# Cached values of sample batches 3 to 7 loaded from the scalar engine's DMA queue in a two-layer streaming encoder step

## What is computed

```python
def attn_mixer_sample(h, ck, cv, cki, w_in, q_g, k_g, w_out):
    ...
    k_all = jnp.concatenate([ck, k], axis=1)
    v_all = jnp.concatenate([cv, v], axis=1)
    ki_all = jnp.concatenate([cki, ki], axis=1)
    k_sel = min(TOPK_MAX, (P + T) // 4)
    o = sparse_attend(q, qi, wi, pos, k_all, v_all, ki_all, k_sel)
    return o @ w_out, k, v, ki
```

## Time and profile before

| | |
|---|---|
| Time before, median of 3 runs | 1678.91 us (1678.46 to 1679.55) |
| Profiled execution, its own time | 1676.94 us |
| Span of its trace | 1675.0 us |
| PE busy | 1617.9 us, 97% of the span |
| DVE, ACT, POOL busy | 55%, 37%, 10% of the span |
| HBM read over the span | 136.29 MB |
| Scores of batch 0 begin | 219.58 us into the span |
| Scores of batch 7 begin | 269.87 us |
| Scores of prompt block 1 begin | 278.69 us |
| Last output transposed | 338.05 us |

### The profile page before, as it was taken

How to read it: one execution, slowest core, us unless ns; L and a number is a source line. 1 busy time by engine, 2 the same in 40 slices (tenths; PEclk the granted TensorE clock), 3 DMA queues, 4 the chain that set the end, 5 groups by cost and what they waited for, 6 DMA issues and landing times.

```text
span 1675.0 us, 25851 instructions
## 1 busy us (share of the span) xinstructions
PE 1617.9 (97%) x11138; PEld 1548.9 (92%) x11138; DVE 927.9 (55%) x1287; ACT 621.4 (37%) x928; POOL 168.1 (10%) x270
## 2 busy tenths in 40 slices
PE   7999878999999999999999999999999999999998
PEld 7759835799999999999999999999999999999998
DVE  5278877445665266526656715537663566346653
ACT  4546434734332133213354433324331233123441
POOL 2000000012110011001121100021110011001200
PEclk9999989999999999999999999999999999999999
DMA  5212445011222222221231221321222122211321
GB/s 217 80 50 77 153 179 201 26 58 69 76 76 76 76 76 72 80 76 56 75 112 70 92 83 55 113 76 64 72 72 95 52 76 76 101 51 63 114 92 48
DMA packets 27938, 143.52 MB, mean 86 GB/s; under 512 B 3392, under 2 KB 7104, under 8 KB 14640
## 3 DMA queue, kind: packets, MB, share of 16 engines
q1 hardware_dynamic: 26912, 139.03, 23.5%
q0 software_dynamic: 768, 2.81, 0.5%
q10 hardware_dynamic: 144, 0.02, 0.0%
HBM read 136.29 MB, written 5.43 MB: 85 GB/s over the span
## 4 chain that ended last, share of the span: by engine, by line
PE 92%; DVE 3%; ACT 2%; issue 1%; DMA 0%; SPq 0%; ACTq 0%; DVEq 0%
PE psum L634 71%; PE psum L680 9%; PE psum L720 2%; PE psum L551 1%; PE psum L490 1%; PE psum L583 1%; PE psum L499 1%; PE psum L590 1%; PE psum L538 1%; PE psum L669 1%; PE psum L510 1%; PE psum L565 1%; ACT a_hi L973 1%; DMA xT<-in_xT 0%; PE psum L759 0%
## 5 line engine op out<-in xcount | busy, mean ns | idle before, releaser
L634 PE MATMUL psum<-a_hi,w_hi 128*128 128x384 f32 (+2 forms) x1920 | 439.2, 310 | 7.5 <-DVE a_lo L1283 7.5
L634 PE MATMUL psum<-a_hi,w_lo 128*128 128x384 f32 (+2 forms) x1920 | 437.8, 309 | 0.0
L634 PE MATMUL psum<-a_lo,w_hi 128*128 128x384 f32 (+2 forms) x1920 | 437.7, 309 | 0.0
L634 PEld LDWEIGHTS psum<-a_hi,w_hi 128*128 128x128 f32 x1920 | 341.8, 188 | 9.6 <-issue 6.7
L634 PEld LDWEIGHTS psum<-a_hi,w_lo 128*128 128x128 f32 x1920 | 342.3, 188 | 0.0
L634 PEld LDWEIGHTS psum<-a_lo,w_hi 128*128 128x128 f32 x1920 | 342.2, 188 | 0.0
L1277 DVE TENSOR_TENSOR w_lo<-w_raw,w_hi 128x2048 fp32r<-128x2048 f32 (+1 forms) x101 | 227.3, 2250 | 120.7 <-ACT w_hi L970 120.6
L970 ACT ACTIVATE w_hi<-w_raw 128x2048 fp32r<-128x2048 f32 (+1 forms) x102 | 189.6, 1858 | 171.8 <-PE psum L634 171.8
L634 PE MATMUL psum<-g_hi,w_hi 128*128 128x320 f32 x832 | 191.2, 311 | 2.4 <-DVE u_act L1489 1.6
L1126 ACT ACTIVATE conv<-conv_in,convw 128x656 f32<-128x656 f32 x88 | 82.4, 937 | 293.4 <-DVE conv_in L1523 293.4
L634 PE MATMUL psum<-g_hi,w_lo 128*128 128x320 f32 x832 | 190.1, 310 | 0.0
(11 more groups left out here) (227 smaller groups left out, 1948.5 us busy)
## 6 DMA issues: line engine op xcount, KB each, us to landing
w_raw<-in_weights SPq DMA_DIRECT2D x93, 1024.0 KB, 4.8
key_b<-in_keyT SPq DMA_DIRECT2D x8, 1024.0 KB, 7.6
val_b<-in_val SPq DMA_DIRECT2D x8, 1024.0 KB, 4.8
w_raw<-in_weights SPq DMA_DIRECT2D x8, 768.0 KB, 4.2
kidx_b<-in_kidxT SPq DMA_DIRECT2D x8, 512.0 KB, 3.6
xT<-in_xT SPq DMA_DIRECT2D x2, 1280.0 KB, 7.1
out_yT<-xT SPq DMA_DIRECT2D x8, 320.0 KB, 2.2
xT<-in_xT SPq DMA_DIRECT2D x3, 640.0 KB, 8.3
```

The lines of the kernel that those rows point to most:

```text
L634: last = pe.matmul(psum[:, 2 * j + bank, 0:t1 - t0], w[:, k, P * j:P * j + P], x[:, k, t0:t1], start=(k == 0 and n == 0), stop=(k == K - 1 ...
```

## The change

The loop on SP issues value loads for batches 0 to 2 alone. For batches 3 to 7 it waits for the logits of batch b - 3 and issues the key load, and nothing else. The value loads of batches 3 to 7, with the small copies, are issued by ACT in `take_out` of batch b - 3, behind the wait for `out_ready` that stands there already. Buffers, transfers, bytes and semaphore counts stay as they are.

```diff
@@ -435,10 +435,9 @@
                 sp.dma_start(key_b[b % KV][:, :, 0:PAST], keyT_in[b]).then_inc(s_key[b % KV], 16)
                 if b == 0:
                     sp.dma_start(onehot[:, :], onehot_in).then_inc(s_onehot, 16)
-                if b >= KV:
-                    sp.wait_ge(out_ready, n_out_ready[S0 + b - KV])
-                sp.dma_start(val_b[b % KV][:, 0:8, :], val_in[b]).then_inc(s_val[b % KV], 16)
-                sp.dma_start(val_b[b % KV][0:TQ, 8, :], vtok[TQ * b:TQ * b + TQ, TT - 1, :]).then_inc(s_val[b % KV], 16)
+                if b < KV:
+                    sp.dma_start(val_b[b][:, 0:8, :], val_in[b]).then_inc(s_val[b], 16)
+                    sp.dma_start(val_b[b][0:TQ, 8, :], vtok[TQ * b:TQ * b + TQ, TT - 1, :]).then_inc(s_val[b], 16)
             sp.wait_ge(logits, n_logits[S1 - 1])
@@ -876,6 +875,10 @@
 
                 kind, a, h = att[s]
                 act.wait_ge(out_ready, n_out_ready[s])
+                if kind == "s" and a + KV < NB:
+                    b = a + KV
+                    act.dma_start(val_b[b % KV][:, 0:8, :], val_in[b]).then_inc(s_val[b % KV], 16)
+                    act.dma_start(val_b[b % KV][0:TQ, 8, :], vtok[TQ * b:TQ * b + TQ, TT - 1, :]).then_inc(s_val[b % KV], 16)
                 o = psum[:, 6 + s % 2, 0:P]
                 act.wait_ge(sum_inverse, n_sum_inverse[s])
```

## The result

| | before | changed |
|---|---|---|
| Median of the runs of the comparison | 1679.55 us (5 runs, 1678.46 to 1681.96) | 1673.13 us (5 runs, 1672.38 to 1673.27) |
| Ratio of changed to before | | 0.9960, 95% interval 0.9945 to 0.9974 |
| Profiled execution, its own time | 1676.94 us | 1673.01 us |
| Span | 1675.0 us | 1671.0 us |
| Mean granted TensorE clock of the profiled execution | 0.988 | 0.988 |

The change makes the kernel 6.4 us faster by the medians, 0.4%, twice what a measurement of this kernel can tell from no change. The 1674.1 us forecast was 1.0 us too high, and the saving of 4.84 us too small by 1.6; the difference between the two, 0.6 us, is that the forecast started from the earlier median of 1678.91.

What follows compares the result with a forecast made beforehand. PE was taken to bound the kernel, idle only where batches 4 to 7 wait for keys; four steps cut from 31.04 to 26.20 us gain 4.84, so 1678.91 - 4.84 = 1674.1 us, range 1671.8 to 1676.6.

Steps and rivals of the forecast that it cites:

- What bounds: Whole kernel: PE holds 92% of the chain; only its idle time ahead of batches 4 to 7 can be won, 4.84 us.
- The four gaps: PE idle ahead of line 548 in batches 4 to 7, 1.62, 0.40, 1.04 and 1.14 us, from late key landings.
- Why the keys were late: SP's key loads: issued some ten us after their buffer is free, then queued behind 1 MB of values issued 0.94 us earlier.
- the 16.6 us of lead: Key loads on SP: 16.6 us from issue to use against landings of 7.3 to 8.1 us, at least 8 us early.
- The cover on ACT: Before ACT's next exponential: 3.65 us idle hides the 0.9 us issue of a value load and its copy.
- rival 3: ACT's issuing delays the exponential beyond 3.65 us a pair; slower kernel from 4.6 us, 1685.8 us at 6; chance 0.05.
- The value loads' lead and the rate of the engines: Sample batches: values have 17.3 us to load; transfers need 322 GB/s against 418 GB/s, 77%, so neither delays a step.
- Rival 1: Key loads: only issue time is saved, at most 0.94 us a gap, 3.2 us in all, 1675.7 us; chance 0.04.
- Rival 2: TensorE clock falls once more (1675.8 us, chance 0.12) or once less (1672.3 us, chance 0.10), 1.75 us a fall.
- Rivals 3 and 4: ACT becomes the bound, slower (0.05); or another wait replaces the gaps or keys weren't their cause, 1676.5 to 1679 us (0.08).

Runs made afterwards that it cites:

- experiment 1: Against the kernel before: all loads on SP, key b issued ahead of value b - 2, no wait in front of the keys; 1673.97 us, ratio 0.9963.
- Experiment 3: Against the kernel before: all loads on SP, wait for `out_ready` kept, next batch's keys issued ahead of the values; 1673.72 us, ratio 0.9962.
- Experiment 4: Changed kernel with each value load of batches 3 to 7 cut into 16 or 8 loads on ACT; 1689.69 us (16), 1673.96 us (8).
- experiment 2: Changed kernel with SP's wait for `out_ready` put back ahead of the next keys, values still on ACT; 1680.10 us, ratio 0.9998 to before.
- the kernels without gaps: The changed kernel and the two one-queue kernels on SP with keys ahead of values; 22 executions, 1673.4 us on average, clock 0.9867.
- 8 pieces: Changed kernel with each value load of batches 3 to 7 issued by ACT as 8 loads of 128 KB; 1673.96 us, ratio 0.9971 to before.

## Why the prediction was right, and where it was off

**What bounds.** Right. The four gaps were the keys' landing; they went when the keys were early, and a step is 6.55 us. From batch 2 to 7 the saving against the first profile of before is 4.83 in both profiles of the changed kernel and 4.84 and 4.83 us in experiments 1 and 3.

**Why the keys were late.** Half right. I named two causes, the wait at line 439 and the values in front in transfer. Experiment 3 keeps the first and has the whole gain, experiment 1 removes both. Only the transfer in front had to go. The prediction said that the gap would close wholly "not in part" from the 16.6 us of lead, which was true; it did not see that 0.9 us of lead and first place in the queue would have done.

**The cover on ACT.** Right in kind and size: a pair is 0.85 to 1.0 us (0.34 and 0.51 to 0.65), expected 0.9; idle time ahead of the exponential 2.74 to 2.88 us, expected 2.7. No output, exponential or maximum was late. The price at which rival 3 begins was too low: I let the exponential cost time from 3.65 us of issuing on, though I had found 1.04 us between it and the next scores. Experiment 4 shows the sum of the two, 4.7 us.

**The value loads' lead and the rate of the engines.** Right: no wait ahead of L589, the products with the values.

**Rival 1, issue time alone.** Out. The rule of the Trainium skill behind it, "DMA: Bandwidth & Descriptors", section "Issuing engines are not separate DMA queues", agrees with experiment 2: two queues at the same time, 430 GB/s, keys after 7.9 to 9.5 us, and no gain. It says nothing against a change in which the second queue frees the first from a wait.

**Rival 2, the clock.** This is the term that was mis-sized. I set the falls before and after as a lottery with a mean of nothing, "I see no reason for the change to move that difference", and took the profile's 1.97 us below the median as chance. Over 59 and 22 executions its mean was not nothing: the kernels without gaps have a granted clock higher by 0.0011, and that fits the 1.35 us that the gaps' own 4.85 don't explain. That the forecast came within 1.0 us of the median is in part luck, since it left this term out and began from a median of before that was 0.6 us lower. Where it is won stays open. A fall in the gaps points the right way, but one of the three profiles of before has it, and experiment 2; the other way point two falls that none of the three profiles of before has. One is behind batch 7, in the profiles of the changed kernel and of experiments 1, 2 and 3. The other reaches into 225 to 230 us, in all eight profiles of the other kernels, with gaps or without, and it stands ahead of every load that they issue at another time or from another queue (229.9 us in the changed kernel); what brings it is open. All three profiled executions of before (1675.2 to 1677.9) lie below its median, so no profile shows a typical one. The waits tested here say nothing more on it.

In the first profile of each kernel other falls hid this. Behind batch 7 the changed kernel was 4.61 us ahead (274.08 against 278.69). It then had falls at 273 to 277 and 338 to 342 us, where before had them at 400 and 1017, and the spans end 4.0 us apart. Each of these falls lasts so long at half speed that 1.7 us of full speed are lost where nothing covers it.

**Rivals 3 and 4.** The first costs time from an issue time of about 4.7 us a batch on (experiment 4), and would make the kernel slower than before from about 4.7 + 4.84 / 5 = 5.7 us, an estimate; the second did not come up.

## What to carry to other kernels

When a load is late, look at what is in transfer in front of it and beside it before moving it to another queue: two loads issued at the same time on two queues share the same engines, and here the urgent one landed no sooner than behind the other on one queue. Issue the urgent load first, or early, and put waits for later events behind it. The mean granted clock of the kernels with and without gaps differed here by what is worth over 1 us, beside a change worth 4.8, so compare it over many executions before a single profile's difference is explained.

## What was not expected of the hardware

- Two 1 MB loads issued 0.2 us apart on SP's and ACT's queues: the keys, issued first, landed after 9.5 us and the values after 7.2. One behind the other on SP's queue it was 4.7 to 4.9 for the first and 6.7 to 9.0 for the second, over three profiles.
- A small copy behind a load on ACT's queue, 0.51 to 0.68 us as a rule, took 2.04 us once (experiment 2) and 1.29 once (8 pieces); ACT's next copy out of PSUM came right behind it. It is not ACT's queue alone: on SP's, two of the five copies of experiment 3 took 2.19 and 1.87 us.
- The same gap can be followed by a fall of the clock or not: the clock fell at the 2.11 us gap behind batch 7 in both profiles of the changed kernel and in that of experiment 2, and in none of the three of before, whose gap is the same.
